# The opening of a two-layer decoder kernel: loads in another order, row loads on GpSimd, and matmuls of ones moved between the transposes

## The reference

```python
for layer in range(DEPTH):
    h = rms_norm(x, norm_mix[layer])          # x * rsqrt(mean(x*x) + eps) * gain
    proj = h @ w_in[layer]
    (a_qkv, a_beta, a_alpha, a_gate, b_q, b_f, b_i, b_gate, c_qkv, br_gate) = jnp.split(proj, offsets, axis=-1)
    # gated DeltaNet, HGRN2 and dilated attention, gated and summed, w_out, residual
    h = rms_norm(x, norm_ffn[layer])
    # layer 0: dense SwiGLU; layer 1: top 2 of 8 SwiGLU experts
```

## Time and profile before

| | us |
|---|---|
| median of three runs | 2060.42 |
| the profiled execution's own time | 2065.84 |
| its span | 2064.0 |
| PE busy in the span | 2024.1 |
| DVE busy | 1580.3 |
| ACT busy | 1249.8 |
| granted TensorE clock, mean of the span | 0.991 |

### The profile page before, as it was taken

The page is one execution under the profiler, slowest core; times in us unless marked ns, Lnnn a source line. Parts: engine busy times, 40 slices in busy tenths (PEclk is TensorE's granted clock), DMA queues, the critical chain, the costliest instruction groups (busy, mean ns, idle before and its releaser), DMA issues.

```text
span 2064.0 us, 28723 instructions
## 1 busy us (share of the span) xinstructions
PE 2024.1 (98%) x10749; PEld 1729.1 (84%) x10749; DVE 1580.3 (77%) x1218; ACT 1249.8 (61%) x1066; POOL 13.9 (1%) x21
## 2 busy tenths in 40 slices
PE   9999999999999999999999999999999999999998
PEld 8988878789998988888777888888888888888887
DVE  4777955765445777955767898898989889898987
ACT  4665455444334565455446777777777777777775
POOL 0000000000000000000000000000000000000000
PEclk9999999999999999999999999999999999999999
DMA  7532455345554532455348999999999999999996
GB/s 257 165 100 90 142 176 183 102 155 188 187 184 143 184 103 82 143 166 182 104 170 296 380 354 379 372 357 379 358 381 354 378 371 355 379 358 379 356 375 243
DMA packets 240765, 516.59 MB, mean 250 GB/s; under 512 B 11528, under 2 KB 34312, under 8 KB 240686
## 3 DMA queue, kind: packets, MB, share of 16 engines
q1 hardware_dynamic: 238274, 507.39, 69.4%
q0 software_dynamic: 2144, 7.88, 1.1%
q10 hardware_dynamic: 268, 0.22, 0.0%
HBM read 513.35 MB, written 2.12 MB: 250 GB/s over the span
## 4 chain that ended last, share of the span: by engine, by line
PE 91%; DVE 5%; issue 2%; ACT 2%; DVEq 0%; ACTq 0%
PE PS L480 27%; PE PS L482 26%; PE PS L481 26%; PE PS L564 7%; PE PS L1085 1%; ACT hi L1208 1%; PE PS L1048 1%; PE PS L802 1%; PE PS L716 0%; DVE lo L1707 0%; DVE t_n L1730 0%; DVE stat L2121 0%; PE PS L1036 0%; DVE b_gc L2040 0%; PE PS L671 0%
## 5 line engine op out<-in xcount | busy, mean ns | idle before, releaser
L1707 DVE TENSOR_TENSOR lo<-raw,hi 128x2048 fp32r<-128x2048 f32 x481 | 1095.9, 2290 | 300.1 <-ACT hi L1208 297.4
L1208 ACT ACTIVATE hi<-raw 128x2048 fp32r<-128x2048 f32 x481 | 919.7, 1915 | 317.1 <-PE PS L482 308.6
L480 PE MATMUL PS<-hi,e_hi 128*128 128x512 f32 x896 | 355.1, 396 | 1.4 <-DVE e_lo L1730 1.4
L482 PE MATMUL PS<-hi,e_lo 128*128 128x512 f32 x896 | 349.5, 390 | 0.0
L481 PE MATMUL PS<-lo,e_hi 128*128 128x512 f32 x896 | 349.0, 389 | 0.0
L480 PE MATMUL PS<-hi,actT_hi 128*128 128x512 f32 x640 | 253.9, 397 | 3.7 <-DVE lo L1707 3.1
L482 PE MATMUL PS<-hi,actT_lo 128*128 128x512 f32 x640 | 249.6, 390 | 0.0
L481 PE MATMUL PS<-lo,actT_hi 128*128 128x512 f32 x640 | 249.1, 389 | 0.0
L480 PE MATMUL PS<-hi,fT_hi 128*128 128x512 f32 x536 | 208.7, 389 | 0.0
L482 PE MATMUL PS<-hi,fT_lo 128*128 128x512 f32 x536 | 208.7, 389 | 0.0
L481 PE MATMUL PS<-lo,fT_hi 128*128 128x512 f32 x536 | 208.6, 389 | 0.0
(11 more groups left out here) (332 smaller groups left out, 2128.7 us busy)
## 6 DMA issues: line engine op xcount, KB each, us to landing
raw<-in_moe_w SPq DMA_DIRECT2D x336, 1024.0 KB, 6.2
raw<-in_w_in SPq DMA_DIRECT2D x92, 1024.0 KB, 5.1
raw<-in_ffn_w SPq DMA_DIRECT2D x33, 1024.0 KB, 5.3
raw<-in_w_br SPq DMA_DIRECT2D x12, 1024.0 KB, 5.0
raw<-in_w_out SPq DMA_DIRECT2D x8, 1024.0 KB, 5.0
hankel<-hankel_dram POOLq DMA_DIRECT2D x1, 1536.0 KB, 9.9
x<-in_x SPq DMA_DIRECT2D x2, 512.0 KB, 5.4
f_gain<-in_norm_ffn POOLq DMA_DIRECT2D x2, 512.0 KB, 3.8
```

The source lines that it names most:

```text
L480: pe.matmul(out, a_hi, b_hi, start=first, stop=False, skip_group_check=True)
L482: return pe.matmul(out, a_lo, b_hi, start=False, stop=last, skip_group_check=True)
L1208: act.activation(hi[prog.u % SPLIT][:, :], raw[slot][:, :], COPY).then_inc(hi_made.sem, 1)
L1707: dve.tensor_tensor(lo[prog.u % RAW][:, :], raw[prog.u % RAW][:, :], hi[s][:, :].bitcast(F32), ALU.subtract).then_inc(lo_made.sem, 1)
```

## The change

It edits the opening alone, in five places.

1. SP's loads: half 0 of x goes ahead of the identity, and both count on one semaphore, `x_here[0]`, for which ACT waits with 32. The gain has `first_here` for itself, and PE waits for it with 16.
2. The seven small loads into `rows` are issued from POOL's queue ahead of the two `hankel` transfers, and no more from ACT's.
3. ACT's function table is loaded without waiting for DVE's constants.
4. On PE the block of 22 matmuls of ones becomes 4; the spread of the gain follows; then 6 once the first half of x and the identity have landed.
5. Seven matmuls of ones stand between the transposes of token tile 0 and those of tile 1. The eight at the end of `parameters()` are gone. All of them now write bank 3.

```diff
-        def turn_input(tile, phase, L, b):
+        def turn_input(tile, phase, L, b, fill=0):
...
             for k in range(KT):
                 turn(0, k)
+            ones_pass(fill)
...
+        def ones_pass(count):
+
+            for _ in range(count):
+                mm(PS[:, 3, 0:P], ones, ones)
+
         pe.wait_ge(tiny_made.sem, 5)
-        for _ in range(22):
-            mm(PS[:, 7, 0:P], ones, ones)
-
-        pe.wait_ge(first_here.sem, 32)
+        ones_pass(4)
+        pe.wait_ge(first_here.sem, 16)
...
-            for _ in range(8):
-                mm(PS[:, 0, 0:P], ones, ones)
...
             if L == 0:
-                pe.wait_ge(first_here.sem, 32)
-            turn_input(hn, 0, L, 0 if L else 4)
+                pe.wait_ge(x_here[0].sem, 32)
+                ones_pass(6)
+            turn_input(hn, 0, L, 0 if L else 4, fill=0 if L else 7)
...
-                act.wait_ge(x_here[t].sem, 16)
+                act.wait_ge(x_here[t].sem, 16 if t else 32)
...
-        for r, src in rows_of_small:
-            load(rows[r:r + src.shape[0], :], src, rows_here)
+        load_tables()
         act.wait_ge(tiny_made.sem, 4)
-        load_tables()
...
+        for r, src in rows_of_small:
+            pool.dma_start(rows[r:r + src.shape[0], :], src).then_inc(rows_here.sem, 16)
         pool.wait_ge(params_kept.sem, 1)
...
-        load(consts[:, K_ID, :], dram["masks"][:, K_ID, :], first_here)
-        for t in range(TT):
-            load(x[:, t, :], xr[t], x_here[t])
+        load(x[:, 0, :], xr[0], x_here[0])
+        load(consts[:, K_ID, :], dram["masks"][:, K_ID, :], x_here[0])
+        load(x[:, 1, :], xr[1], x_here[1])
```

More of the change, by code:

```diff
@@ L2446, in _ @@
     def _(pool):
+        rows_of_small = (
+            (R_CONV, dram["conv_a"].rearrange("l t (c p) -> (l t c) p", p=P)),
+            (R_LB, dram["lb_logits"].rearrange("l (h p) -> (l h) p", p=P)),
+            (R_GA, dram["gnorm_a"]), (R_GB, dram["gnorm_b"]),
+            (R_QN, dram["qnorm_c"].rearrange("l g p -> (l g) p")),
+            (R_KN, dram["knorm_c"].rearrange("l g p -> (l g) p")),
+            (R_FN, dram["norm_ffn"][1:2, :].rearrange("l (k p) -> (l k) p", p=P)))
+        assert len(rows_of_small) == N_ROW_LOADS
+        for r, src in rows_of_small:
+            pool.dma_start(rows[r:r + src.shape[0], :], src).then_inc(rows_here.sem, 16)
         pool.wait_ge(params_kept.sem, 1)
```

## The result

The changed kernel took 2067.32 us, the median of 20 runs (2065.39 to 2069.83). The kernel before took 2061.10 in 20 runs beside it. The ratio is 1.0027, with a 95% interval from 1.0020 to 1.0034: about 5.6 us slower, inside the half per cent that the prediction called no change. The forecast was 2055.6 with a range up to 2062.0; the time lies 11.7 us above the one and 5.3 above the other. The profiled execution took 2066.68 us, and its span is 2064.9.

The account below looks back on a forecast made before the run. PE was taken to bound the kernel, with 91% of the chain of waits. `group_T` 6.75 us earlier, less 1.9 of clock, gave 4.8 us; off the median 2060.42 that is 2055.6, range 2051.0 to 2062.0.

Parts of the forecast that it names:

- given back: Rival, chance 0.12: PE comes 5 us earlier to the third weight unit or DVE, which does not come earlier; 2060.4 us.
- Spread of the gain: PE's opening: four ones end at 3.55 us, the gain has landed by then, and its spread runs to about 7.2.
- cold rival: Rival, chance 0.20: the one-row spread does not keep the clock, so PE's opening runs at half clock; 0.5 us gained, 2059.9.
- ACT and DVE: Opening: DVE starts `hn` of tile 0 at 7.4 us; `hi` of the first weight unit starts at 11.49.
- the good side's bound: Opening: the first unit and x half 1 may land earlier with ACT's small loads gone; 1.5 us allowed.
- The first rise of the clock: PE's opening: full clock for the seven ones between the transposes, 14 x 0.12 = 1.7 us, ending at 11.5.
- The fall of the clock: Around `group_T`'s start: clock lost for a mean 4.8 us, costing 2.4 against 0.5 before; net 1.9 us lost.
- The opening's net: Opening: `group_T` starts 6.75 us earlier, at 16.7, less 1.9 us of clock: 4.8 us gained.
- Taking the 4.8 off the median: Whole kernel: the profiled execution took 2065.84 us, but the 4.8 was taken off the median 2060.42, giving 2055.6.
- Row loads on POOL: POOL's opening: seven issues at 0.80 us each, landed at 11.7, ahead of PE's need at 14.6.
- the slower rival: Rival, chance 0.06: POOL's row loads land at 25.0, PE waits at `rows`; 3.9 us slower, 2064.3.

Follow-up runs that it names:

- e6: The kernel before, unchanged, timed and profiled once more; the profiled execution took 2056.82 us, and its runs form groups with medians 2060.0 and 2065.7.
- e1: The changed kernel plus 106 already satisfied waits (53 instructions) on PE in the router stage, restoring the expert loop's place: 2058.27 us, ratio 0.9983.
- e3: The changed kernel plus 52 satisfied waits (26 instructions) on PE in the router stage: 2057.86 us, ratio 0.9977.
- e4: As e3, but with the identity loaded ahead of half 0 of x again: 2057.03 us, ratio 0.9970.
- e5: As e3, but with the seven row loads issued from ACT's queue again: 2058.04 us, ratio 0.9981.
- e10: As e4, but with 3 instead of 6 ones behind the gain and 76 satisfied waits instead of 52: 2057.95 us, ratio 0.9977.
- e7: As e3, without the 6 and the 7 ones, and with 104 satisfied waits at the norm of layer 1 in their place: 2062.34 us, ratio 1.0002.
- e9: The kernel before plus 512 satisfied waits (256 instructions) on PE in the router stage: 2081.86 us, one execution.
- e2: The kernel before with 9 instead of 22 matmuls of ones ahead of the gain's spread: 2067.47 us, ratio 1.0031.
- e8: The kernel before plus 406 satisfied waits (203 instructions) on PE in the router stage: 2089.07 us, one execution.

## Why the prediction was wrong

**The step that failed** is the first sentence of its argument: "a microsecond taken off PE's queue in the opening is a microsecond at the end, unless a later wait gives it back". I looked for waits on data. What gave it back was the place of the expert loop's code, which moved because matmuls were taken out of a straight piece of code 1100 us earlier. The prediction has no term for instruction fetch and no rival for it. Its "given back" rival had the right kind of outcome, but named the third weight unit and DVE, and neither held PE up; the fetch at the two jumps back did, for 8.55 us. Such a term could not be read from waits of before, as before has none. But the size of the loop in packets can be counted from the code, and its even steps of 121.08 us in before show that it ran unhurt: a loop that large, with instructions taken away ahead of it, was a rival worth pricing.

**Spread of the gain.** Predicted from 3.5 to about 7.2, measured from 3.85 to 7.63. Right. But the 7.2, from which the cold rival counts too, was a guess at the spread's length, and no run shows it: the four instructions took 1.98 us in before, at a granted clock of 1.00, and 3.78 here, at the pace of 0.21 us for one of ones. DVE, which in before had waited 9.79 us for PE ahead of `hn`, waited 5.84 here.

**ACT and DVE.** `hn` of tile 0 predicted at 7.4, measured 7.75; `hi` of the first unit 11.49, measured 10.57, because its load landed 0.9 us earlier (the good side's bound).

**The first rise of the clock.** Predicted ahead of the seven ones, which are counted at 0.12 us each, measured 13.49, inside them. This step was wrong. I had gone by the rise at 7.43 in before, where ones from 1.84 on stood ahead; here eight of ones and four of one row did. The one-row matmuls kept PE busy for 3.78 us and did not bring the rise; this is the "cold" rival's premise, and it was half right, as all up to 13.49 ran at half clock. So the six ones and the first transposes took 2.9 and 1.7 us. The 9.8 at which the prediction has these transposes end no run shows; they ended at 12.19.

**The fall of the clock.** Predicted around the first L480, with 1.9 us lost in `group_T`. It did not fall. This was wrong too, against the late rise the other way: `picks` took the 2.02 us of the full clock, and all of `group_T` had it. The two errors nearly cancel, which is luck: first L480 at 17.34 for 16.7. What I read from the earlier trace rows, that transposes and `picks` lose the clock, is true of an opening where DVE's `hn` makes PE pause 1.55 us; after has no such pause. There, transposes and `picks` ran from 14.43 to 17.32 and the clock stayed at 1.00. By these two openings the pause goes with the fall; no run took the pause alone away.

**The opening's net.** Forecast 4.8 us, measured 5.8 against the same execution by `f_gain` at 412 us. Right in kind, 1.0 too small.

**Taking the 4.8 off the median** was a second mistake, a smaller one. The profiled execution was of before's upper group, whose opening is 4.3 us longer at 413 us than that of the other (e6). Against that one the change wins 1.6 us by `f_gain`, not 5.8, and by 1133 it is 1.2 behind (1133.16 against 1131.96), since the changed kernel's clock was 0.89 in both norm stretches where that one had 1.00. How much of the norms' falls is the change's and how much chance stays open: the six profiles with the changed opening and its ones (after, e1, e3, e4, e5, e10) show 0.89 to 0.91 at both norms, and the four with that of before anything from 0.77 to 1.00. The 10 to 12 runs each of e3 and e1 put the gain of the opening at about 3 us of the median, which is some 2 us against before's faster group and 7.5 against its slower one. Even without the loop's loss the time would have been 2057.9 to 2058.3 (e3, e1), some 2.5 us over my 2055.6 and inside the range.

**Row loads on POOL.** Predicted 0.80 us an issue, measured 0.50 to 0.73; no wait at `rows`. Right, and the slower rival falls.

**Sum:** 7.5 us won by 1133, of which 5.8 by 412, and 8.55 lost in the loop. Put right by 26 or 53 instructions of satisfied waits, the same change is a gain of 0.17 to 0.23%.

## What to carry to other kernels

Where a kernel has a long loop on TensorE (this one is some seven packets of code), any edit ahead of it, even one that only removes instructions, can add fetches to each pass: count the packets in the row of the instruction queue of both profiles, look for idle time put down to issue, and look how long the loop's jump takes in PE's queue (0.21 us or 4.81 here). A wait that the profile puts down to data, right behind a jump, can be the same fetch. If the count rises, shift the loop by some satisfied waits in a place where the engine is idle before judging the edit itself; where it isn't idle, the waits cost time themselves, as in e7. And when a sum is taken off a median, first find out whether the profiled execution is like the median run, by a second profile of the same kernel.

## What the hardware showed unexpectedly

- A loop of about 1766 PE instructions ran its passes without one packet of code in before, e1, e3 and e9, and with 18 more packets in after and e2. Each of the two jumps back took 4.7 to 5.7 us in after, e2 and e8 instead of 0.21, and the step is 4.1 to 4.3 us longer (5.8 in e8, where the clock fell as well). The nine packets of a pass come all through it, and only the first two hold PE up. Why nine, and where in the first 26 instructions the edge lies, stay open.
- Two satisfied waits share one instruction (106 waits in e1 are 53 records). Of these, 53 in an idle place cost 0.3 us altogether, and 52 in one that is not idle took 5.5 us.
- The matmuls of one row (128 columns of ones by a row of 512) took 0.95 us an instruction at the lower clock and left the clock there for as long as they ran.
- The same opening of the same kernel lost the clock for 3.42 us in one execution and 10.24 in another, 4.3 us apart at 413 us.
- The function table's load (1.28 us, from 1.95), the DMA issues on ACT (0.26 to 1.12 us each) and those on POOL (0.50 to 0.73) were all covered in the opening.
